# A three-layer block: recurrence with early parameter columns, seams by blocks, turned narrow projections and another order in the first attention

## The chip, the cores and the metric

The kernel runs on one core of one Trainium2 chip. The metric is the device time of one execution in microseconds. TensorE multiplies, VectorE, ScalarE and GpSimd work elementwise, SyncE issues most transfers; each engine runs its own list of instructions in order, and they wait for one another by semaphores. Three runs of the kernel before took 1351.91, 1352.85 and 1360.21 us, median 1352.85.

## The reference, cut to what matters

256 tokens of width 1024, float32, batch 1. Three layers in a row.

```
# layer 1: complex diagonal recurrence (32 groups, 16 channels, 64 states), then an MLP
u = rms(h) @ w_in                      # 1024 -> 512
x[t] = a * x[t-1] + B u[t]             # complex, per group; a, B from lam, dt
y = Re(C x) + d * u
z = gelu(y); z = z * sigmoid(z @ w_glu); mix = z @ w_out
h = h + rms(mix)
h = h + rms(relu(rms(h) @ w1)**2 @ w2) # 1024 -> 4096 -> 1024
# layer 2: attention over selected keys, then an MLP of the same shape
q, k, v, qi, ki, wi = split(rms(h) @ w_in)   # 1024, 256, 256, 512, 64, 8 columns
q, k, qi, ki = rope(each)
score[t, s] = sum_heads relu(qi . ki) * wi   # 8 heads
keep the 64 keys of highest score (causal); softmax attention, 16 heads on 4 of k, v
h = h + rms(o @ w_out); h = h + rms(MLP(rms(h)))
# layer 3: one projection (z, conv part, dt: 32 columns, q, k, v, gates), a chunked
# state recurrence and three dilated window attentions side by side, then a conv FFN
dt = softplus(proj_dt + bias)
```

## The kernel before, in words

Activations are kept as two blocks of 128 tokens (`tb`). Every weight comes in **pieces** of 1 MB, each of two halves a and b, by SyncE into `raw` (two buffers). ScalarE copies a half rounded into `HI` (`hi_next`, `hi_to`), and the difference raw - HI goes to `LO`: half a by VectorE (`lo_next`, `lo_to`), half b by GpSimd (`upto`), both by `low_part`; `lo_both` is VectorE doing both. `HI` and `LO` have four slots; a slot is free when TensorE signals `piece_done`, and a buffer of `raw` is free when the difference of the piece two before is taken. A product is three matmuls (`three`: high x high, high x low, low x high). Activations are split in the same way after being turned: TensorE transposes `y` in four quarters (block, half of the columns) into PSUM (`norm_transpose`), ScalarE takes the high part `XH` (`xT_high`), VectorE the low part `XL` (`xT_low`).

The order of the work is written out by hand, one list for each engine; `keep_busy` puts matmuls on zeros between, here called fillers. No planner orders anything.

**Recurrence** (0 to 107 us). VectorE makes the tables from the parameters: powers, then `w5` (B times powers), angles and their fraction of a turn in `e5`, `cq5` (C times powers). Parameters that lie in rows are turned into columns (`late_columns`, in the middle of `inputs_turned`). TensorE projects u in two pieces (`ch_major`), ScalarE reorders it (`to_steps`) and copies the turned tables (`inputs_out`), takes sine and cosine. TensorE makes `kernels5` and four `drive`s; VectorE scans four groups (`scanned`); `within` and `carried` give y; ScalarE's gelu, then `glu` and the down projection.

**Seam** between two layers: `post` squares the result (ScalarE), scales it (VectorE), takes the power -0.5 (GpSimd, `row_rstd`) and adds it to `h`; `pre` squares h, takes the power and writes `y`. In the kernel before, `post` runs over both token blocks, then `pre` over both, then the four quarters. TensorE has 20 fillers ahead of the transposes and 2 between the blocks. The last down piece of an MLP signals `acc_first` when its token block 0 is complete.

**First attention**. Pieces from number 37 (`P_ATT`): two for the index queries, a narrow one of 72 columns (ki, wi: the tail), two for k and v, two and two for q, four for the output. `tok_major` with n < 128 runs 48 matmuls of n columns with four fillers. The index scores of block 0 are summed and its 64 largest found (8 turns of MAX8 and MATCH_REPLACE8), then those of block 1; `rotate_keys` comes before, `rotate_queries(0)` between. Twelve jobs follow (`JOBS1`): scores, masked maximum (`largest1`), exponential, division (`normed1`), transpose, weighted sum.

**Start of layer 3**. Nine projections c of two pieces each for q, v, k, each 48 matmuls of 512 columns, into PSUM banks `bank2(c)`; c = 0 and c = 1 share banks 0 and 1, since the narrow dt projection (32 columns, piece 84) has bank 2. `head_norm` normalises q and k heads; `softplus` follows c = 0.

## Time and profile before

| | |
|---|---|
| median of 3 runs | 1352.85 us |
| profiled execution | 1348.93 us |
| its span | 1347.1 us |
| TensorE busy | 1299.1 us (96%) |
| VectorE busy | 985.8 us (73%) |
| ScalarE busy | 667.3 us (50%) |
| GpSimd busy | 434.8 us (32%) |
| mean granted clock | 0.991 |

The times of the trace are counted from the first instruction; the profiled execution's own time is 1.8 us longer than its span. A busy TensorE can be running fillers. A granted clock of 1.00 is 2.4 GHz, 0.50 is 1.2 GHz; a stretch between them holds both. A matmul's duration in a row is its latency, matmuls overlap: their spacing is read from the starts.

### The profile page before, as it was taken

How to read it: one execution, taken by the hardware profiler on the slowest of the kernel's cores; microseconds unless marked ns; L12 is line 12 of the kernel's file. 1: busy time of each engine (PE TensorE's matmuls, PEld its weight loads, DVE VectorE, ACT ScalarE, POOL GpSimd, SP SyncE). 2: the span in 40 equal slices, each digit the busy share in tenths (PEclk: the TensorE clock that was granted, in tenths of full speed). 3: DMA queues.
4: the chain of work that ended last, by engine and by line, in shares of the span. 5: the costliest groups of instructions: out<-in, count | busy, mean ns of one | idle time of the engine just before them, and what ended most of it. 6: DMA issues, size and time to landing. Idle time of an engine off the chain costs nothing.

```text
span 1347.1 us, 21106 instructions
## 1 busy us (share of the span) xinstructions
PE 1299.1 (96%) x7798; PEld 1101.8 (82%) x7798; DVE 985.8 (73%) x1486; ACT 667.3 (50%) x1119; POOL 434.8 (32%) x213
## 2 busy tenths in 40 slices
PE   6999999999999999999999999999999979999998
PEld 6876888878667788887888888899999947899998
DVE  7977777676964755556665645499999985699997
ACT  5755444444464544445354544355555523455553
POOL 3005444544201555554354322210000002345553
PEclk9999999999889999999899999999999999999999
DMA  7026665645203566663465533354454314366663
GB/s 227 17 85 200 189 197 184 190 134 188 94 32 125 157 191 189 191 193 108 156 209 162 151 94 95 92 150 136 141 155 141 125 63 141 90 191 189 187 187 109
DMA packets 166363, 197.12 MB, mean 146 GB/s; under 512 B 9981, under 2 KB 131325, under 8 KB 166269
## 3 DMA queue, kind: packets, MB, share of 16 engines
q1 hardware_dynamic: 164939, 191.54, 46.4%
q10 hardware_dynamic: 1362, 4.74, 1.0%
q8 instruction: 40, 0.66, 0.2%
q14 instruction: 22, 0.18, 0.0%
HBM read 195.20 MB, written 1.05 MB: 146 GB/s over the span
## 4 chain that ended last, share of the span: by engine, by line
PE 71%; DVE 20%; issue 3%; ACT 3%; DMA 1%; POOL 1%; DVEq 0%; SPq 0%; ACTq 0%
PE acc L639 21%; PE wk L594 9%; PE wk L571 7%; PE wk L573 7%; PE wk L572 7%; PE wk L596 4%; DVE LO L1844 4%; DVE arena L2376 2%; PE acc L618 2%; PE wk L1075 1%; PE acc L571 1%; PE acc L1101 1%; PE acc L572 1%; PE acc L573 1%; DVE arena L2375 1%
## 5 line engine op out<-in xcount | busy, mean ns | idle before, releaser
L447 POOL TENSOR_TENSOR LO<-raw,HI 128x1024 fp32r<-128x1024 f32 (+1 forms) x160 | 401.1, 2512 | 830.9 <-ACT HI L1320 789.3
L1320 ACT ACTIVATE HI<-raw 128x1024 fp32r<-128x1024 f32 (+3 forms) x382 | 364.5, 996 | 115.7 <-DMA raw<-in_w_in 27.4
L447 DVE TENSOR_TENSOR LO<-raw,HI 128x1024 fp32r<-128x1024 f32 (+1 forms) x160 | 221.6, 1388 | 114.3 <-ACT HI L1320 113.9
L571 PE MATMUL wk<-X,HI 128*128 128x256 f32 x784 | 224.6, 286 | 2.0 <-DVE X L1877 1.2
L572 PE MATMUL wk<-X,HI 128*128 128x256 f32 x784 | 221.7, 283 | 0.0
L573 PE MATMUL wk<-X,LO 128*128 128x256 f32 x784 | 221.7, 283 | 0.0
L594 PE MATMUL wk<-X,HI 128*128 128x512 f32 x512 | 182.3, 399 | 2.5 <-DVE X L1877 2.5
L571 PEld LDWEIGHTS wk<-X,HI 128*128 128x128 f32 x784 | 150.2, 192 | 5.0 <-issue 2.8
L572 PEld LDWEIGHTS wk<-X,HI 128*128 128x128 f32 x784 | 150.3, 192 | 0.9
L573 PEld LDWEIGHTS wk<-X,LO 128*128 128x128 f32 x784 | 150.2, 192 | 0.0
L596 PE MATMUL wk<-X,LO 128*128 128x256 f32 x512 | 143.5, 280 | 0.0
L639 PE MATMUL acc<-HI,HH 128*128 128x512 f32 x424 | 131.9, 392 | 3.8 <-DVE HL L2419 3.1
L639 PE MATMUL acc<-LO,HH 128*128 128x512 f32 x424 | 131.0, 390 | 0.0
L639 PE MATMUL acc<-HI,HL 128*128 128x512 f32 x424 | 130.8, 390 | 0.0
L594 PEld LDWEIGHTS wk<-X,HI 128*128 128x128 f32 x512 | 96.2, 188 | 26.4 <-issue 2.9
L596 PEld LDWEIGHTS wk<-X,LO 128*128 128x128 f32 x512 | 96.6, 189 | 1.1
L571 PE MATMUL wk<-HI,X 128*128 128x512 f32 (+2 forms) x240 | 93.3, 389 | 1.6 <-DVE arena L2303 1.5
L639 PEld LDWEIGHTS acc<-LO,HH 128*128 128x128 f32 x424 | 79.6, 188 | 17.3
L639 PEld LDWEIGHTS acc<-HI,HL 128*128 128x128 f32 x424 | 79.6, 188 | 17.0
L572 PE MATMUL wk<-LO,X 128*128 128x512 f32 (+2 forms) x240 | 91.1, 380 | 0.0
L573 PE MATMUL wk<-HI,X 128*128 128x512 f32 (+2 forms) x240 | 91.1, 379 | 0.0
L639 PEld LDWEIGHTS acc<-HI,HH 128*128 128x128 f32 x424 | 75.4, 188 | 18.8 <-DVE HL L2419 4.0
(364 smaller groups left out, 2158.1 us busy)
## 6 DMA issues: line engine op xcount, KB each, us to landing
raw<-in_mlp_w SPq DMA_DIRECT2D x128, 512.0 KB, 4.0
raw<-in_w_in SPq DMA_DIRECT2D x100, 512.0 KB, 3.9
raw<-in_w_up SPq DMA_DIRECT2D x44, 512.0 KB, 3.9
raw<-in_w_down SPq DMA_DIRECT2D x44, 256.0 KB, 3.1
raw<-in_att_w_in SPq DMA_DIRECT2D x16, 512.0 KB, 4.4
raw<-in_w_ssd_proj SPq DMA_DIRECT2D x16, 512.0 KB, 4.2
raw<-in_att_w_out SPq DMA_DIRECT2D x8, 512.0 KB, 4.4
raw<-in_w_out SPq DMA_DIRECT2D x8, 512.0 KB, 4.3
```

Of the source, the lines that this page charges most:

```text
L447: tensor_tensor(LO[:, s, cs], raw[:, s % 2, "ab".index(part), 0:m], HI[:, s, cs].bitcast(F32), ALU.subtract).then_inc(S(f"lo_{part}"), 1)
L571: mm(o, lh, rh, start=start, stop=False, skip_group_check=skip)
L572: mm(o, lh, rl, start=False, stop=False, skip_group_check=skip)
L573: return mm(o, ll, rh, start=False, stop=stop, skip_group_check=skip)
L594: mm(o, HI[:, s, w:w + P], X2[:, k, :, :].rearrange("p r t -> p (r t)"), start=k == 0, stop=False, skip_group_check=True)
L596: last = mm(o[:, 0:SEQ], LO[:, s, w:w + P], XH[:, k, :], start=False, stop=k == KD - 1, skip_group_check=True)
L618: mm(o, zero_bf[:, 0:P], zero_bf[:, :], start=True, stop=True, skip_group_check=True)
L639: last = mm(acc[:, tb, n * 512:(n + 1) * 512], lhs[:, ts], w[:, s, c:c + 512], start=begin, stop=end, skip_group_check=True)
L1075: last = mm(wkf[:, o:o + K], qT2[hs, gi * 4 + hd // 2, tb * P:(tb + 1) * P], kT2[hs, gi * 4 + hd // 2, 0:K], start=True, stop=True)
L1320: A(HI[:, s, j * m:(j + 1) * m], raw[:, s % 2, j, 0:m], ACT.Copy).then_inc(S(f"hi_{part}"), 1)
L1844: TT(LO[:, s, cs], raw[:, s % 2, "ab".index(part), :], HI[:, s, cs].bitcast(F32), ALU.subtract).then_inc(S(f"lo_{part}"), 1)
L2376: STT(o, x, taps[j][k], o, ALU.mult, ALU.add)
```

## The change

Four things, in one diff.

**Recurrence.** GpSimd waits for the first turned activations before its half of piece 0 and takes both halves of piece 1. VectorE computes the small tables ahead of `xT_low(0)`; all four products of `w5` come before the four sums. The columns are turned ahead of the second projection. The products `kernels5` are cut in halves, one ahead of the last six `inputs_turned`, one behind `drive(0)`. ScalarE copies `cq5` into place; VectorE makes the third copy in `e5`. ScalarE's order becomes u, columns, u, both `inputs_out`. Fillers are fewer: 130 before, 101 after.

**Seams behind both MLPs.** `post` and `pre` go block by block; the last two down pieces run block 0 of both, then block 1 of both; block 0's transposes and projection come before block 1's transposes.

**Turned narrow projections.** The 72 and the 32 columns become the stationary operand, 24 matmuls of 256 columns, and are transposed back.

**First attention.** k, v and q projections of the tail's successors are cut by token block; both blocks' scores are summed before the keys are rotated; four `rel` buffers; jobs 0 and 1 begin inside the search of block 1; second query half rotated inside jobs 0 and 1. GpSimd waits at four places for VectorE's rotations. In layer 3, c = 1 has its own banks and `softplus` follows c = 3.

```diff
 gpsimd, recurrence
+            pool.wait_ge(S("xT_hi"), 1)
             upto(0)
+            pool.wait_ge(S("lo_a"), 1)
+            pool.wait_ge(S("tables5"), 1)
+            low_part(pool, G.tensor_tensor, Ring().at(1), "a", 2048)
+            upto(1)
 gpsimd, first attention
-            row_rstd(3)
-            row_rstd(4)
+            row_rstd(3, 4)
+            upto(P_ATT + 4)
+            pool.wait_ge(S("ki_roped"), 2)
+            upto(P_ATT + 6)
+            pool.wait_ge(S("lo_a"), P_ATT + 8)
+            upto(P_ATT + 8)
+            pool.wait_ge(S("q_roped"), 2)
+            upto(P_ATT + 10)
+            pool.wait_ge(S("q_roped"), 4)
             upto(P_ATT + 14)
 tensor
+            def ch_narrow(s, o, n):
+                for k in range(KD):
+                    last = three(o, HI[:, s, k * n:(k + 1) * n], LO[:, s, k * n:(k + 1) * n], XH[:, k, :], XL[:, k, :],
+                                 k == 0, k == KD - 1)
+                return last
+            def back_turned(src, dst, n):
+                for tb in range(TB):
+                    last = nc.tensor.transpose(dst(tb), src[:, tb * P:(tb + 1) * P], ident[0:n, 0:n])
+                return last
...
             pe.wait_ge(S("ct_ready"), 1)
+            pe.wait_ge(S("cols_ready"), 2)
-            keep_busy(spare5, 4)
-            for g in range(8):
+            keep_busy(spare5, 2)
+            inputs_turned(0)
+            inputs_turned(1)
+            keep_busy(spare5, 2)
+            pe.wait_ge(S("w5_ready"), 2)
+            kernels5(0)
+            for g in range(2, 8):
                 inputs_turned(g)
                 keep_busy(spare5, 2)
...
+            drive(0)
+            keep_busy(spare5, 2)
+            pe.wait_ge(S("dd5_ready"), 1)
+            kernels5(1)
+            for q in range(1, 4):
+                keep_busy(spare5, 1)
                 drive(q)
...
-            for q, n in enumerate((0, 4, 10, 10)):
+            for q, n in enumerate((0, 1, 2, 5)):
                 keep_busy(spare5, n)
                 carried(q)
-            keep_busy(spare5, 8)
+            keep_busy(spare5, 5)
...
-            keep_busy(spare5, 14)
+            keep_busy(spare5, 7)
             glu(glu_slot, 2)
...
-            norm_transpose(2, 20, 2)
-            proj1(0, 0, 2)
-            proj1(0, 1, 2)
+            norm_transpose(2, 14, 0, (0, 1))
+            slots = [arrived(), arrived()]
+            for tb in range(TB):
+                if tb == 1:
+                    norm_transpose(2, 0, 0, (2, 3))
+                for part in range(2):
+                    last = tok_block(slots[part], wk[:, tb, :], tb, 4 * part, 4, 512, part == 0, part == 1, 2)
...
             s = arrived()
-            used(tok_major(s, lambda tb: wk[:, 2 + tb, 0:ATT_TAIL], 0, KD, ATT_TAIL, True, True))
+            used(ch_narrow(s, accf[0:ATT_TAIL, 1024:1024 + SEQ], ATT_TAIL))
+            s = arrived()
+            tok_block(s, wk[:, 2, :], 0, 0, 4, 512, True, False)
+            pe.wait_ge(S("tail_read"), 1)
+            back_turned(tailT, lambda tb: tail1[:, tb, 0:ATT_TAIL], ATT_TAIL).then_inc(S("tail_psum"), 1)
+            used(tok_block(s, wk[:, 3, :], 1, 0, 4, 512, True, False))
 scalar, first attention
+            hi_to(P_ATT + 4)
+            done(P_ATT + 2)
+            A(tailT, accf[0:ATT_TAIL, 1024:1024 + SEQ], ACT.Copy).then_inc(S("tail_read"), 1)
             hi_to(P_ATT + 6)
             tile_evac(0, qiT[:, :, 0:P])
 vector
+            def by_block(j, e, n):
+                scaled(j, e, 0)
+                residual(e, 0)
+                pre_block(n, e + 1, 0)
+                scaled(j, e, 1)
+                xT_low(n, (0, 1))
+                residual(e, 1)
+                pre_block(n, e + 1, 1)
+                xT_low(n, (2, 3))
...
+            summed(0)
+            summed(1)
+            rotate_keys()
+            lo_to(P_ATT + 7)
+            searched(0)
+            lo_to(P_ATT + 8)
+            rotate_queries(0)
+            searched(1, first_jobs)
             for n in range(N1 + 1):
                 if n + 2 < N1:
                     largest1(n + 2)
-                if n in (N1 - 2, N1 - 1):
+                if n < TB:
+                    rotate_queries(1, (n,))
+                if n in (2, 3, N1 - 2, N1 - 1):
                     lo_next()
-                if n + 1 < N1:
+                if 1 <= n < N1 - 1:
                     normed1(n + 1)
```

ScalarE's `by_block` has the order: squares of the result for block 0, of h for block 0, of the result for block 1, `xT_high` of quarters 0 and 1, squares of h for block 1, `xT_high` of quarters 2 and 3.

## Rows read from the trace of the kernel before

**Rows 1.** The page: busy time by engine; shares of the chain that ended last.
```profile
PE 1299.1 (96%) x7798; PEld 1101.8 (82%) x7798; DVE 985.8 (73%) x1486; ACT 667.3 (50%) x1119; POOL 434.8 (32%) x213
...
PE 71%; DVE 20%; issue 3%; ACT 3%; DMA 1%; POOL 1%; DVEq 0%; SPq 0%; ACTq 0%
```
**Rows 2.** Stretches of TensorE: length, busy, granted clock, DMA share, GB/s.
```profile
298.00:306.60 8.60, 7.48 (x40) 1.00 0.00 1
360.70:370.90 10.20, 9.81 (x34) 0.54 0.01 2
650.70:657.50 6.80, 5.31 (x23) 0.57 0.01 2
654.54:667.54 13.00, 13.00 (x50) 0.85 0.11 26
```
**Rows 3.** Timeline of VectorE, recurrence: start us, duration us, line, form, idle before.
```profile
15.72 2.22 DVE L1928 TENSOR_TENSOR arena<-arena 128x16 f32<-128x16 f32 x1
...
26.47 2.36 DVE L1844 TENSOR_TENSOR LO<-raw,HI 128x1024 fp32r<-128x1024 f32 x2
...
57.75 0.69 DVE L2036 TENSOR_TENSOR arena<-wk,arena 128x512 f32<-128x512 f32 x1 [1.23 <-PE wk L720]
...
79.46 2.35 DVE L1844 TENSOR_TENSOR LO<-raw,HI 128x1024 fp32r<-128x1024 f32 x2
```
**Rows 4.** Timeline of GpSimd, recurrence.
```profile
15.56 2.35 POOL L447 TENSOR_TENSOR LO<-raw,HI 128x1024 fp32r<-128x1024 f32 x1 [4.37 <-ACT HI L1320]
```
**Rows 5.** Timeline of ScalarE, recurrence: second `to_steps`, second gelu.
```profile
44.53 4.46 ACT L1399 ACTIVATE y<-wk 32x128 f32<-32x128 f32 x16
...
82.61 4.47 ACT L1456 ACTIVATE arena<-acc 32x128 f32<-32x128 f32 x16 [2.65 <-PE acc L748]
```
**Rows 6.** Timeline of TensorE, recurrence: `kernels5`, `drive`, last `carried`, fillers ahead of `glu`.
```profile
47.24 0.97 PE L730 MATMUL acc<-arena 128*128 128x32 f32 x8
...
60.04 1.90 PE L720 MATMUL wk<-y,arena 128*128 128x64 f32 x16
...
80.68 1.89 PE L748 MATMUL acc<-arena 128*128 128x63 f32 x16
...
87.44 3.19 PE L618 MATMUL acc<-zero_bf 128*128 128x512 bf16 x14
```
**Rows 7.** Timeline of VectorE: last hidden low part of the first MLP.
```profile
289.97 0.69 DVE L2114 TENSOR_TENSOR HL<-arena,HH 128x512 fp32r<-128x512 f32 x1 [0.70 <-ACT HH L1489]
```
**Rows 8.** Timeline of TensorE: first matmul behind the first seam.
```profile
306.60 0.47 PE L571 MATMUL wk<-HI,X 128*128 128x512 f32 x1
```
**Rows 9.** Stretches of TensorE: 48 matmuls of 256 columns; the 72-column tail.
```profile
22.00:27.86 5.86, 5.86 (x51) 1.00 0.51 183
317.60:323.60 6.00, 6.00 (x54) 1.00 0.60 177
```
**Rows 10.** Timeline of TensorE: first matmul of c = 1.
```profile
654.54 0.79 PE L571 MATMUL wk<-HI,X 128*128 128x512 f32 x1 [1.49 <-DVE arena L2303]
```
**Rows 11.** Timeline of ScalarE behind the seam: pieces 39 and 40, then 41.
```profile
307.54 2.68 ACT L1320 ACTIVATE HI<-raw 128x288 fp32r<-128x288 f32 x4 [0.33 <-issue]
314.75 1.06 ACT L1320 ACTIVATE HI<-raw 128x1024 fp32r<-128x1024 f32 x1 [4.53 <-DMA raw<-in_att_w_in]
```
**Rows 12.** Timeline of TensorE: query transposes; transposes of the fifth job.
```profile
360.68 1.17 PE L859 MATMUL acc<-cst,arena 128*128 128x128 f32 x8 [2.68 <-ACT arena L1522]
...
393.80 0.66 PE L939 MATMUL acc<-cst,arena 128*128 128x128 f32 x4
```
**Rows 13.** Timeline of VectorE: query rotation until the next sum; search of block 1.
```profile
353.22 0.68 DVE L453 TENSOR_TENSOR y<-wk,cst 128x512 f32<-128x512 f32 x1
...
357.44 0.35 DVE L2192 TENSOR_SCALAR arena<-arena,wi_s 128x256 f32<-128x256 f32 x1
...
361.80 0.43 DVE L2200 MAX8 top<-arena 128x8 f32<-128x256 f32 x1
...
369.67 0.29 DVE L2203 TENSOR_SCALAR arena<-arena 128x256 bf16<-128x256 f32 x1
```

More of the change, by code:

```diff
@@ L87, in next, with at @@
         return s, k, n
+    def at(self, n):
+        while self.n < n:
+            self.next()
+        return self
     def enter(self, i, per_slot):
@@ L602, in tok_major, with tok_block @@
                 for tb in range(TB):
-                    for k in range(kt):
-                        ts = slice(tb * P, (tb + 1) * P)
-                        if norm is not None:
-                            xT_wait(norm, tb, k0 + k)
-                        if n < P and k % 4 == 0:
-                            keep_busy(accf[:, 1536:2048], 1)
-                        last = three(outs(tb), XH[:, k0 + k, ts], XL[:, k0 + k, ts], HI[:, s, k * n:(k + 1) * n],
-                                     LO[:, s, k * n:(k + 1) * n], start and k == 0, stop and k == kt - 1)
+                    last = tok_block(s, outs(tb), tb, k0, kt, n, start, stop, norm)
                     if tb == 0 and first:
                         last.then_inc(S(first), 1)
+                return last
+            def tok_block(s, o, tb, k0, kt, n, start, stop, norm=None):
+                ts = slice(tb * P, (tb + 1) * P)
+                for k in range(kt):
+                    if norm is not None:
+                        xT_wait(norm, tb, k0 + k)
+                    last = three(o, XH[:, k0 + k, ts], XL[:, k0 + k, ts], HI[:, s, k * n:(k + 1) * n],
+                                 LO[:, s, k * n:(k + 1) * n], start and k == 0, stop and k == kt - 1)
                 return last
@@ L643, in down, with norm_transpose @@
                 return last
-            def norm_transpose(n, meanwhile=0, between=0):
+            def norm_transpose(n, meanwhile=0, between=0, quarters=range(4)):
                 keep_busy(wk[:, 3, :], meanwhile)
-                for q in range(4):
+                for q in quarters:
                     tb, b = q // 2, q % 2
@@ L722, in drive, with kernels5 @@
                 last.then_inc(S("bu_psum"), 1)
-            def kernels5():
-                for i in range(ST):
-                    if i % 2 == 0:
-                        keep_busy(spare5, 1)
+            def kernels5(half):
+                for i in range(8 * half, 8 * half + 8):
+                    keep_busy(spare5, 1)
                     for r in range(2):
@@ L839, in mlp @@
                 mlp_up(MC - 1, 1)
[L840 to L841 removed]
+                slots = []
+                for tb in range(TB):
+                    for par in range(2):
+                        if tb == 0:
+                            pe.wait_ge(S("hid_lo"), MC - 1 + par + base)
+                            slots.append(arrived())
+                        ts = slice(tb * P, (tb + 1) * P)
+                        for kk in range(2):
+                            for lhs, w, end in ((HH, HI, False), (HH, LO, False), (HL, HI, par == 1 and kk == 1)):
+                                for n in range(2):
+                                    c = kk * 1024 + n * 512
+                                    last = mm(acc[:, tb, n * 512:(n + 1) * 512], lhs[:, par, kk, ts], w[:, slots[par], c:c + 512],
+                                              start=False, stop=end, skip_group_check=True)
+                        if tb == 1:
+                            used(last)
+                    if tb == 0:
+                        last.then_inc(S("acc_first"), 1)
             mlp(0)
[L846 removed]
+            norm_transpose(2, 14, 0, (0, 1))
             def proj1(bank, part, norm=None):
@@ L1869, in pre, with xT_low @@
                     pre_block(n, e, tb)
-            def xT_low(n):
-                for q in range(4):
+            def xT_low(n, quarters=range(4)):
+                for q in quarters:
                     tb, b = q // 2, q % 2
```

335 lines of the change are left out of this document (186 added, 149 removed).

## The prediction, made blind

> **What bounds the kernel.** I read the page first: TensorE is busy 96% of the span and holds 71% of the chain that ended last, VectorE 20% [rows 1]. Matmuls set the time nearly everywhere, so only places where TensorE waits, runs fillers (`keep_busy`) or has its clock lowered can give anything. The stretches by window show where: the granted clock is 0.54 to 0.57 (for most of the stretch the lower level, 1.2 GHz) in a stretch of 10 us of the first attention and in one of 7 us at the start of layer 3; at the seams it stays at the upper level, 2.4 GHz [rows 2]. Then the timelines of each engine, for five places: the recurrence (0 to 107 us), two seams (298 and 627 us), the first attention (307 to 430 us) and the two narrow projections in it and behind 646 us. In the recurrence VectorE runs from 10 to 80 us with hardly a pause: the reader sees it wait for TensorE's drives (1.23 us), the longest of its pauses there [rows 3]. The MLPs, the second attention and the chunked recurrence are untouched; what is gained ahead of them should arrive at the end, since they are bound by TensorE.
>
> **Recurrence, -4.7 us (bounds -1 and -6).** Removed from VectorE: two differences of piece 1 (2.3 us) and a stall in which a subtraction on 16 elements took 2.22 us while GpSimd subtracted 1024 columns [rows 3, 4]. GpSimd now waits for the first turned activations (about 17.1 us) and then subtracts 0b; a VectorE instruction with two SBUF operands stops for it again, for about 1 us. So I get: small block from 15.9 to 20.5, low parts of the activations and piece 0 to 24.1, powers (2.8 us) to 26.9, where the tables before began at 28.9. GpSimd's two halves of piece 1 (2.4 us each) run to about 33. The first four table products read PSUM, which the rows show unhindered; the four sums behind them lose some 1.5 us. Tables, angles and inner products then end at about 51.
>
> That is not what the scans wait for. Piece 0 is projected 24.2 to 30, the late columns and eight fillers reach 32, piece 1 runs 33.1 to 38.9 (both projections at 5.8 us). ScalarE takes 4.5 us for u's second half [rows 5], then eight copies paced by TensorE, for half of the kernel products (8 x 0.6 us, from four of them in 0.8 [rows 6] and a filler each) stand between: to 51.0; absolute value, sine, cosine (3.1 us) to 54.1; VectorE's added copy 0.7 us to 54.9. Before, the first scan began at 57.75. The second needs drive 1, now behind the second half of the products: 51.0 + 1.7 for drive 0, 0.4 fillers, 5.0 products, 1.0 skip term, 0.2, 1.7 for drive 1 [rows 6] = 61.0 us. Three scans of 5.43 us follow: 77.4 instead of 79.5 us. Fewer fillers (10 + 10 ahead of the last two `carried` become 2 + 5, 14 ahead of the third glu group become 7) let TensorE follow at once: last `carried` ends at 79.7 instead of 82.4, ScalarE's second gelu (4.5 us) and copy at 84.8, low part at 85.5, third glu group at 85.6 instead of 90.3 [rows 5, 6]. That is 4.7 us, and the down projection inherits it. The four copies of `cq5` moved to ScalarE (4 us) lie before the products' end, in its free time. If they or the sine chain end later than I have them, the gain shrinks to 1.
>
> **Seams, -1.0 each (bounds +1 and -3).** The last two down pieces are run block by block: block 0 is complete 24 matmuls (5.5 us) before the end instead of 12, but its second half needs the last hidden low part, which ends at 290.66 [rows 7] where TensorE would be at 289.8: 0.9 us of wait, MLP end 299.0. Block 0: squares, power, residual, squares, power, product: y at 300.6. Fourteen fillers (3.0 us) hold TensorE to 302.0 and hide it. Transposes, ScalarE's and VectorE's copies: first matmul at 303.75 instead of 306.60 [rows 8]. But block 1's residual now stands on VectorE behind block 0's low parts: its y comes at 308.8, its activations at 311.1, while block 0's 24 matmuls end at 309.3. Turning, 0.9 us more wait, 5.6 us: 316.7 instead of 317.7. The second seam has the same instructions.
>
> **Narrow projections: -3.0 in the attention, -6.7 with what follows in layer 3.** 48 matmuls of 72 or 32 columns take 0.11 us each whatever their columns, with four fillers 6.0 us; 48 matmuls of 256 columns take 5.8 us [rows 9]. Turned: 24 of these, 2.9 us, and two transposes, 0.3: -3.0 for 72 columns, -3.3 for 32, which began to run at the low clock. ScalarE's copy lies beside the next matmuls. Bounds: no gain, and -4. Behind 646 us two things go as well: c=1 no longer waits for head_norm 0 (1.49 us [rows 10]), since its banks are free, and its 48 matmuls no longer start at the low clock (13.0 us [rows 2] against 11.1 between seam and tail [rows 8, 9], -1.9). Softplus (9 us of VectorE) moves to c=3, where VectorE has only differences; pieces lead by three there. Total here -6.7; bounds -4 and -8.
> What the Trainium skill says speaks against turning: by "TensorE: Matmul & The Clock Gate", section "Back-to-back issue gap", an isolated matmul costs its streamed columns, N/2.4 + 2.5 ns with a floor near 25, so 1.2 us before and 2.6 us after; the same section says that a stream with weight loads is slower than that at small N, and the 0.11 us above agree with the latter.
>
> **First attention, -4.6 with its tail's 3.0 (bounds +3 and -6).** The 3.0 us won in the tail are at once at risk. HI of pieces 39 and 40 was taken right behind the seam at 307.5; now ScalarE is in the seam until 311. Piece 41 can load when 39 is split, 43 when 41 is; ScalarE takes 43 ahead of the first evacuation. Pieces took 3.5 to 6 us from a freed buffer, with two in flight [rows 11]: I get HI 43 ready at about 329, where TensorE stands at 326.5: 2.8 us of wait. Then key projection and index products to 342, last value half 344.7. VectorE sums both blocks' scores first (to 344.4) and only then turns the keys (3.3 us, to 347.7): 3.0 us of wait for TensorE, the successor of the 2.68 us before the query transposes [rows 12]. From there VectorE is the chain: difference 1.2, search of block 0 6.3, difference 1.2, queries 4.1 (360.5), search of block 1 8.6 [rows 13] with the first two jobs inside (3.6), two query rotations and three maxima: third job's product ready at 379.8 instead of 382.2. Two differences stand in jobs 2 and 3 now, but late_queries comes a job later, when its input is there. Fifth job's transposes: 388.2 instead of 393.8 [rows 12], -5.6 against before, of which 1.0 is the seam's: -4.6. From job 4 on both kernels take 3.0 us a job.
>
> **Sum**: 4.7 + 1.0 + 4.6 + 1.0 + 6.7 = 18.0 us. The profiled run took 1348.93 us, 0.3% under the median of 1352.85: 1331 on its scale, **1335 us** for a median.
>
> **Rivals.**
> 1. *The ring starves the attention* (0.20). The wait for piece 43 and the one for the keys are each as long as the 2.68 us behind which the clock fell for 10 us before. Cold stretches on the chain, at 0.43 instead of 0.22 us a matmul, take 3 to 5 us: attention gives 0, sum 13: 1340. For: the chain of loads. Against: all of it is worked out from landings in one profile.
> 2. *ScalarE becomes the recurrence's bound* (0.12): sine behind the eight copies, scans at 57 again, 1 us there: 1339.
> 3. *The narrow matmuls cost their columns* (0.02): at 0.23 us for 512, 32 columns cost 0.014, 48 of them 0.7 us, turned 2.8: two gains of 3.2 become losses of 2.1: 1346. Rows 9 speak against. This is the skill's rule for the isolated gap.
> 4. *Better than worked out* (0.12): seams whose y overtakes the fillers and a piece 43 in time, some 1.5 + 1.5 + 4: 1328.
> 5. *Slower* (0.04): of 130 fillers in the recurrence 29 go. If the clock falls there at about 50 us and stays at half to 105, then the 11 us of down, 5.8 of glu and some 8 of `within` and `carried` double: +25 - 18 = +7, 1360. It decides if the granted clock is low for over 40 us ahead of the MLP. Against: the seams, with as many gaps, stay at 1.00 [rows 2].
>
> **Numbers.** My forecast 0.50 (own range 1330 to 1340). The range 1325 to 1346 takes in rivals 1 to 4 and the bounds. A change of over 1% is 13.5 us, about what this measurement tells from none: faster 0.72 (forecast, rival 4 and some of 1 and 2), same 0.25, slower 0.03.
>
> **What would show it.** Recurrence: first scan at 55, second at 61, first matmul of the MLP 5 us earlier. Seams: TensorE's first block projection 4.8 us behind the last down matmul and a second wait near 1 us. Attention: an idle of TensorE ended by ScalarE's first evacuation, one ended by VectorE's key rotation. Second block: no clock under 1.00 at 645. Wrong if the recurrence gives under 2 us, or if attention's tail gain is kept whole.

## The result: 5.3 to 8.5 us faster, where 18 were forecast

Eight runs of the changed kernel have a median of **1344.15 us** (1341.87 to 1347.69), eight of the kernel before beside them 1352.69 us: ratio 0.9938, 95% interval 0.9909 to 0.9967. A second comparison (e1, below) gave medians 5.3 us apart and 0.9964 (0.9949 to 0.9978). The time lies in the range 1325 to 1346, but the gain is under half of the 18.0 us of the sum, and with under 1% it falls where the prediction had put a chance of 0.25 ("same"), not 0.72. One execution of e5 (3654 us) and one of the kernel before beside e13 to e15 (1370 us) were disturbed and are in no ratio. The profiled execution is the slowest of its eight: 1347.69 us, span 1345.8, against 1347.1 before. It shows where gains arise and go, not their median size.

The page: TensorE is as busy as before, VectorE has 38 us more (not more work: the same 160 splits of one group take 1.65 instead of 1.39 us on average, 263 us instead of 222), and TensorE's share of the chain went from 71% to 68% [rows 1].

```profile
PE 1286.8 (96%) x7700; PEld 1096.1 (81%) x7700; DVE 1024.0 (76%) x1483; ACT 670.9 (50%) x1124; POOL 419.1 (31%) x215
...
PE 68%; DVE 21%; ACT 4%; issue 3%; DMA 2%; POOL 1%; DVEq 0%; SPq 0%; ACTq 0%
```

Stretches of the changed kernel (bounds, length, busy time of PE, PEld, DVE, ACT, POOL, granted clock, DMA share, GB/s). First the first MLP's start, then the first attention behind its narrow projection and three parts of it, layer 3 from its first projection to the second attention, and the latter's start.

```profile
113.00:123.00 10.00, 8.77 (x41) 7.11 (x41) 6.32 (x7) 5.56 (x7) 5.82 (x2) 0.83 0.73 231
...
317.20:438.30 121.10, 108.07 (x532) 82.19 (x531) 76.82 (x221) 58.17 (x130) 28.31 (x13) 0.93 0.32 103
325.00:332.00 7.00, 5.01 (x20) 4.01 (x21) 1.45 (x1) 2.49 (x5) 2.85 (x2) 0.76 0.87 278
347.50:363.00 15.50, 15.43 (x63) 12.93 (x64) 14.54 (x46) 5.53 (x7) 7.29 (x4) 0.80 0.44 137
384.00:396.00 12.00, 9.50 (x53) 7.31 (x54) 5.50 (x19) 7.65 (x20) 2.34 (x1) 0.84 0.44 166
646.20:750.90 104.70, 102.17 (x513) 85.94 (x511) 77.88 (x134) 56.01 (x68) 48.35 (x19) 1.00 0.61 191
...
750.00:762.00 12.00, 10.81 (x52) 9.15 (x53) 7.01 (x14) 5.42 (x11) 2.45 (x1) 0.72 0.42 117
```

The waits of TensorE in the changed kernel (what waited, what ended it, total, times, longest). The three with one occurrence of 3.5, 3.3 and 2.5 us are all in the first attention; before, its one long wait was 2.68 us [rows 12].

```profile
PE acc L921 <- DVE arena L474: 3.5, 1, 3.5
PE acc L921 <- ACT arena L1630: 3.3, 1, 3.3
PE acc L1018 <- DVE arena L2355: 3.2, 3, 1.9
...
PE wk L664 <- ACT arena L1665: 2.5, 1, 2.5
```

Set side by side, the start of each stage tells where time goes. In us from the span's start, read from the timelines of TensorE; "again" is the changed kernel's second trace:

```
                                     before   changed   again
recurrence, down projection starts    97.51    92.65    92.49
first MLP, first matmul              119.47   114.73   114.49
  its second projection              125.80   122.61   120.91
first MLP, last down matmul ends     298.1    296.0    294.4
layer 2, first projection ends       317.7    314.4    312.7
narrow projection ends               323.7    317.2    315.6
attention's output ends              438.3    438.2    440.1
layer 3, first projection ends       646.5    646.1    648.1
second attention starts              756.4    750.9    755.0
span                                1347.1   1345.8   1347.3
```

The changed kernel is 6.5 and 8.1 us ahead behind the narrow projection, and level and 1.8 us late at the end of the attention. All that is won before 317 us is lost in that one stretch: 114.6 us before, 121.1 and 124.5 now. Layer 3 then gives 5.2 and 3.1 us. From the start of the second attention to the end, where nothing was changed, both traces lose again: 590.7 us before, 594.9 and 592.3 now. Of the fifteen other traces (the kernel before and e2 to e15), thirteen have 590.6 to 590.9 and two (e10, e15) 592.2. The second attention's first 12 us run at clock 0.72 in the first trace, at 0.86 in e1, e10 and e15, at 1.00 in the rest. So part of what the first trace lacks is chance.

### The profile page after: what moved, and what is told of

Read it like the earlier page. It is cut to its first block, busy times and chain, and to the rows that moved or that the text cites. A ratio compares the mean times of both kernels' runs of the same rounds, so it can differ in the third digit from the quotient of the medians.

```text
span 1345.8 us, 20924 instructions
## 1 busy us (share of the span) xinstructions
PE 1286.8 (96%) x7700; PEld 1096.1 (81%) x7700; DVE 1024.0 (76%) x1483; ACT 670.9 (50%) x1124; POOL 419.1 (31%) x215
## 3 DMA queue, kind: packets, MB, share of 16 engines
q1 hardware_dynamic: 164939, 191.54, 46.1%
## 4 chain that ended last, share of the span: by engine, by line
PE 68%; DVE 21%; ACT 4%; issue 3%; DMA 2%; POOL 1%; DVEq 0%; SPq 0%; ACTq 0%
PE acc L685 20%; PE wk L637 9%; PE wk L601 6%; PE wk L603 6%; PE wk L602 6%; PE wk L639 5%; DVE LO L1948 4%; DVE arena L2517 2%; PE wk L1163 1%; PE acc L601 1%; PE acc L898 1%; PE acc L1189 1%; PE acc L602 1%; PE acc L603 1%; DVE LO L462 1%
## 5 line engine op out<-in xcount | busy, mean ns | idle before, releaser
L462 POOL TENSOR_TENSOR LO<-raw,HI 128x1024 fp32r<-128x1024 f32 (+1 forms) x162 | 387.5, 2398 | 847.6 <-ACT HI L1408 770.1
L462 DVE TENSOR_TENSOR LO<-raw,HI 128x1024 fp32r<-128x1024 f32 (+1 forms) x160 | 263.3, 1648 | 97.8 <-ACT HI L1408 97.5
L685 PE MATMUL acc<-HI,HH 128*128 128x512 f32 x392 | 122.1, 393 | 3.8 <-DVE HL L2560 3.1
L685 PE MATMUL acc<-LO,HH 128*128 128x512 f32 x392 | 121.3, 390 | 0.0
L685 PE MATMUL acc<-HI,HL 128*128 128x512 f32 x392 | 121.0, 390 | 0.0
L601 PE MATMUL wk<-HI,X 128*128 128x512 f32 x208 | 84.1, 404 | 4.2 <-DVE X L1981 4.2
L685 PEld LDWEIGHTS acc<-LO,HH 128*128 128x128 f32 x392 | 73.6, 188 | 15.9
L685 PEld LDWEIGHTS acc<-HI,HL 128*128 128x128 f32 x392 | 73.6, 188 | 15.8
L2239 DVE TENSOR_TENSOR HL<-arena,HH 128x512 fp32r<-128x512 f32 x32 | 84.0, 2626 | 2.8 <-ACT HH L1601 2.8
L602 PE MATMUL wk<-LO,X 128*128 128x512 f32 x208 | 82.4, 396 | 0.0
```

What stands on the lines that cost most here:

```text
L462: tensor_tensor(LO[:, s, cs], raw[:, s % 2, "ab".index(part), 0:m], HI[:, s, cs].bitcast(F32), ALU.subtract).then_inc(S(f"lo_{part}"), 1)
L601: mm(o, lh, rh, start=start, stop=False, skip_group_check=skip)
L602: mm(o, lh, rl, start=False, stop=False, skip_group_check=skip)
L685: last = mm(acc[:, tb, n * 512:(n + 1) * 512], lhs[:, ts], w[:, s, c:c + 512], start=begin, stop=end, skip_group_check=True)
L2239: TT(HL[:, par, :, :], sq_b[:, par, :].rearrange("p (j t) -> p j t", j=2), HH[:, par, :, :].bitcast(F32), ALU.subtract).then_inc(S("hid_lo ...
```

## The experiments

Two places are given for each: the **attention stretch** (end of the narrow projection to the end of the output) and **layer 3** (end of its first projection to the start of the second attention). Before: 114.6 and 109.9. The ratios are to the kernel before on the same chip.

### e1: the changed kernel again

> The changed kernel once more, nothing altered: a second trace of it, to see which stretches of low clock belong to a place and which come and go. Theory A (the gain is lost in the first attention, by waits that the order of the work makes): the stretch from the last matmul of the narrow projection (317.2 us) to the last matmul of the attention's output (438.4) is again 121 us long, 6 us longer than in the kernel before (114.9), with the same three waits of TensorE of about 3.3, 3.5 and 2.5 us. Theory B (the gain is eaten by chance drops of the clock, other ones in each execution): the stretches of low clock at 114, 752, 1087 and 1097 us lie elsewhere or are missing, and the span is up to 5 us shorter. Both can hold. Ratio to the kernel before 0.994.

Measured: 1344.44 us, ratio 0.9964 (0.9949 to 0.9978); 124.5 and 106.8 us. The three waits return, 3.2, 3.5 and 2.5 us. The low clock at 114 us does not: the MLP's first projection takes 5.9 us and not 7.3. The one at 752 us does, weaker (0.86 against 0.72). Both theories hold in part. The attention's loss belongs to the place, 6.5 to 9.9 us; which stretches outside it run at the lower level changes from one execution to the next.

Four more traces below leave the first attention as it is in the changed kernel: 120.8 (e6), 124.5 (e7), 123.4 (e9) and 124.7 us (e14). So an edit there is told from chance by a single trace only outside 120.8 to 124.7. Layer 3, unaltered in e1 to e6 and e8, takes 104.7 to 107.4.

What a wait costs depends on the clock too. Behind the 2.5 us this trace (timeline of TensorE: start, duration, line, form, idle before) has two jobs at the doubled time:

```profile
389.03 0.38 PE L664 MATMUL wk<-zero_bf 128*128 128x512 bf16 x1 [2.50 <-ACT arena L1665]
389.33 2.07 PE L1009 MATMUL wk<-arena 64*128 64x128 f32 x8
391.33 1.11 PE L1018 MATMUL acc<-cst,arena 128*128 128x128 f32 x4
392.38 1.97 PE L1032 MATMUL acc<-arena 128*64 128x128 f32 x8
...
394.82 2.07 PE L1009 MATMUL wk<-arena 64*128 64x128 f32 x8
```

The score matmuls take 2.07 us where they take 1.16 at the upper level, and the next job's come 5.5 us later instead of 3.0.

### e2, e3, e4: the three waits, one edit each

```diff
 # e2 (VectorE); e3 has it too
             summed(0)
-            summed(1)
             rotate_keys()
             lo_to(P_ATT + 7)
+            summed(1)
 # e3 in addition (ScalarE)
-            hi_to(P_ATT + 6)
+            hi_to(P_ATT + 5)
             tile_evac(0, ...); tile_evac(1, ...); tile_evac(2, ...)
+            hi_to(P_ATT + 6)
 # e4 (ScalarE, alone)
+                if n == 3:
+                    late_queries()
                 if n in (3, 6):
                     hi_next()
-                if n == 3:
-                    late_queries()
```

> VectorE turns the keys and splits the next piece between the two sums of index scores instead of behind both. Theory A: TensorE's wait of 3.5 us ahead of the key transposes (344.1 to 347.6) is gone, the search of block 0 begins 2 to 3 us earlier because the idle time of VectorE inside the second sum is filled, the following 48 matmuls are no longer at the low clock (13.3 to 11.1 us), and the fourth job's transposes come 3 to 5 us earlier; what is left of it at the end of the attention is less, since the fifth job still waits for the late queries: 1 to 4 us. Theory B: no gain, because the wait returns ahead of the query transposes. Ratio 0.991 under A, 0.994 under B.

Measured: 1347.61 us, ratio 0.9971 (0.9943 to 1.0); 128.8 us, longer by 4 than the longest above. The wait ahead of the keys is gone and returns ahead of the query transposes as 5.47 us, with a granted clock of 0.50 from 360 to 370 us. Theory B, and worse than "no gain".

> As the one with the keys first, and ScalarE evacuates the three index transposes before it splits piece 43. Theory A: TensorE's wait of 3.3 us behind the index transposes at 323.7 is gone, and the 12 matmuls behind it take 3.0 us and not 4.1; the index products start 4 us earlier, the sums follow, and the fourth job's transposes come 6 to 9 us earlier than in the changed kernel. Theory B (the ring of pieces sets the pace): the split of 43 only comes a microsecond later and with it pieces 45 to 48, so that TensorE waits as long ahead of the query projections. Ratio 0.988 under A, 0.993 under B.

Measured: 1342.44 us, ratio 0.995 (0.9931 to 0.9968); 120.0 us. The wait behind the index transposes is 0.34 us, the third job's transposes come at 375.1 instead of 379.5 us; 5.46 us of wait ahead of the queries remain. The stretch is 4.5 us shorter than in e1 but only 0.8 under the shortest of the unaltered ones, and the fourth job's transposes came 3.7 us earlier (380.1) where 6 to 9 were expected. Theory A holds for the wait; its size is not shown here. Against e2, which lacks only this edit, the stretch is 8.8 us shorter.

> In the fourth turn of the job loop ScalarE evacuates the late queries before it splits a piece, not behind it. Theory A: TensorE's wait of 2.5 us (387.8 to 390.3) shrinks to about 0.7, the low clock behind it (390 to 393 us) is gone, the fifth job's transposes come 3 us earlier (389 instead of 392.1) and the end of the attention's output 2 to 3 us earlier. Theory B: the jobs behind are bound by VectorE or by GpSimd's split, so that the end of the output stays at 121 us behind the narrow projection. Ratio 0.992 under A, 0.994 under B.

Measured: 1342.86 us, ratio 0.9943 (0.9927 to 0.996); 120.7 us, 3.8 under e1, but no less than e6 has without this edit. The wait is 1.27 us and not the 0.7 expected; e3 and e6, which leave ScalarE's order alone here, have 1.27 and 1.57; the changed kernel, e1, e7, e9 and e14 have 2.5 to 3.7. Fourth to fifth job is still 7.1 us (382.6 to 389.7; 7.0 to 8.4 in the unaltered traces). ScalarE's order is at most a part of this wait; no gain of this edit is shown.

### e5: late queries a job earlier

```diff
 # TensorE: behind the third job, not the fourth
-                if n == 3:
+                if n == 2:
                     late_queries()
 # ScalarE: ahead of copies1(3), not behind hi_next
```

> The late queries are transposed a job earlier, as in the kernel before (behind the third job's transposes and second product), and ScalarE evacuates them ahead of that job's copy. Theory A (the move of this step to the fourth job took its slack: the very next scores need it): no wait of TensorE over 1 us there; from the fourth to the fifth job's transposes 3.0 to 3.5 us instead of 7.0 and 7.5, no low clock behind it, and the attention's output 4 to 6 us earlier measured from the end of the narrow projection (117 us instead of 121.1 and 124.5). Theory B (VectorE or GpSimd bound these jobs): the wait turns up at another job and the stretch stays above 120 us. Ratio 0.991 under A, 0.996 under B.

Measured: 1341.26 us, ratio 0.9899 (0.9865 to 0.9934); 116.9 us, 3.9 under the shortest unaltered one. Theory A, with the number expected: no wait of TensorE over 1 us is left there. Fourth and fifth job's transposes are 3.0 us apart, though this group of late transposes itself still ran at the low clock:

```profile
379.65 1.97 PE L993 MATMUL wk<-cst,arena 128*128 128x128 f32 x8
...
383.43 0.66 PE L1018 MATMUL acc<-cst,arena 128*128 128x128 f32 x4
384.02 1.09 PE L1032 MATMUL acc<-arena 128*64 128x128 f32 x8
385.36 1.16 PE L1009 MATMUL wk<-arena 64*128 64x128 f32 x8 [0.25 <-issue]
386.44 0.66 PE L1018 MATMUL acc<-cst,arena 128*128 128x128 f32 x4
```

### e6: fewer fillers at the seams

```diff
-            norm_transpose(2, 14, 0, (0, 1))     # and (4, 14, ...)
+            norm_transpose(2, 8, 0, (0, 1))      # and (4, 8, ...)
```

> 8 instead of 14 fillers ahead of the first block's transposes at the two seams. In the trace of the changed kernel block 0 of y is ready 1.75 us behind the last down matmul, and the fillers hold TensorE to 3.04. Theory A (the seam gave 0.2 instead of 1.0 us because too many fillers stand in it): the transposes start at 1.75, and the first projection of layer 2 and of layer 3 end 17.1 us behind the last down matmul instead of 18.4: 1.2 us each, ratio 0.994. Theory B (fewer fillers, more idle time, and the clock falls): a granted clock under 1.00 behind the seam, and 1 to 3 us lost: ratio 0.998.

Measured: 1338.99 us, ratio 0.9877 (0.9829 to 0.9925); 120.8 and 104.7 us. The first projection ends 17.2 us behind the last down matmul instead of 18.4, at clock 1.00. The transposes start 2.9 us behind the down matmuls in the changed kernel and 1.6 here:

```profile
295.44 1.68 PE L664 MATMUL wk<-zero_bf 128*128 128x512 bf16 x7
296.95 1.04 PE L701 MATMUL wk<-cst,y 128*128 128x128 f32 x8
299.20 0.47 PE L601 MATMUL wk<-HI,X 128*128 128x512 f32 x1 [1.21 <-DVE X L1981]
```

Theory A in the trace. That the median fell by more than the 2.4 us (0.994 was expected) is not explained; its interval is 13 us wide.

### e7, e9, e14: the wait behind c=2 in layer 3

```diff
 # ScalarE: e7 moves hi_to(last2(1) + 3), three pieces, behind the square; e9 the last piece only:
-                hi_to(last2(c) + 3)
+                hi_to(last2(c) + (2 if c == 1 else 3))
 ...
+                if c == 1:
+                    hi_to(last2(c) + 3)
 # VectorE, e14 in addition to e9
-                lo_to(last2(c) + 3)
+                lo_to(last2(c) + (2 if c == 1 else 3))
                 if not 3 <= c < 6:
                     head_norm(c)
+                if c == 1:
+                    lo_to(last2(c) + 3)
```

> At the start of layer 3 ScalarE squares the projection of c=1 as soon as it is complete, and splits the next pieces behind that. In the traces of the changed kernel the square waited 5.5 us for two transfers that stand ahead of it in ScalarE's order, and TensorE then waited 1.6 and 2.1 us ahead of the transposes behind c=2. Theory A (order on ScalarE): that wait is gone, and c=3 starts 1.6 to 2 us earlier. Theory B (VectorE, which loses 2.3 us to GpSimd in one small instruction, sets it): the wait stays above 1 us. Ratio 0.995 under A, 0.9965 under B.

Measured: 1350.34 us, ratio 0.9954 (0.9919 to 0.9989); layer 3 takes 110.0 us. The wait is gone, and another of 4.36 us stands ahead of c=2's own matmuls, ended by GpSimd's share of their piece: I had moved two pieces that TensorE needed. A miss of the edit, not a verdict on the theory.

> As the square first, but ScalarE still splits two of the three pieces ahead of the square of c=1 and only the third, for which it waited 7.4 us on the transfer, behind it. Theory A (one transfer that nobody needs yet stands ahead of the square): the square starts within 1 us of the end of c=1's projection, c=2's projection does not wait as it did when all three were put behind (4.4 us), TensorE's wait of 1.6 to 2.7 us ahead of the transposes behind c=2 is under 0.3, and the second attention starts 104.5 us or less behind the first projection of layer 3 (before: 109.9, changed kernel: 104.7 and 106.8). Theory B (the collision of VectorE's small instruction with GpSimd alone holds the chain): wait still above 1 us. Ratio 0.9945 under A.

Measured: 1345.55 us, ratio 0.9942 (0.9916 to 0.9969); 106.7 us. The square starts with the end of c=1's projection, and TensorE still waits 1.96 us, where theory A had under 0.3. VectorE had the same late piece ahead of its norm: its split, at 664.6 us, follows an idle of 3.9. GpSimd's subtraction, theory B's cause, is there too: it holds one instruction of the norm for 2.38 us instead of 0.17.

> The changed kernel; at c=1 of layer 3 both ScalarE's square and VectorE's norm stand ahead of the split of the third piece. Theory A (the late piece stands ahead of the norm on two engines): norm of c=1 ready 7 to 9 us behind the end of c=1's projection instead of 13.6, TensorE's wait behind c=2 under 0.3 us, and the second attention 104.5 us or less behind the first projection of layer 3. Theory B (GpSimd's subtraction stops VectorE's small instructions for 2.3 us wherever they stand): the wait is shorter only where no subtraction falls into the norm. Ratio 0.994.

Measured: 1341.25 us, ratio 0.9917 (0.9889 to 0.9945); 102.9 us, no wait behind c=2. ScalarE of e14: the square, then 2.49 us of idle time for the transfer, which nobody waits for any more.

```profile
661.57 1.03 ACT L1731 ACTIVATE y<-wk 128x1024 f32<-128x1024 f32 x1 [3.92 <-PE wk L603]
665.09 1.06 ACT L1408 ACTIVATE HI<-raw 128x1024 fp32r<-128x1024 f32 x1 [2.49 <-DMA raw<-in_w_in]
```

VectorE of e14: the norm of c=1 is complete at 667.5, 6.1 us behind that projection (13.7 in the changed kernel). Theory A gives these numbers, but theory B is not excluded: no subtraction fell into this norm, while in the changed kernel and in e9 one did, for 2.1 and 2.2 us, more than the wait. And e10 below, with e9's order only, shows no wait and 102.9 us as well (e11 and e12, with the same order there: 106.7 and 104.4). The order helps; how much of the wait was the order's and how much GpSimd's is not told apart.

```profile
662.63 1.22 DVE L2442 TENSOR_REDUCE arena<-y 128x16 f32<-128x1024 f32 x1 [0.30 <-ACT y L1731]
...
666.19 1.29 DVE L2446 TENSOR_TENSOR arena<-wk,arena 128x512 f32<-128x512 f32 x2
```

### e8: the waits filled

```diff
+            keep_busy(accf[:, 1024:1536], 14)    # ahead of tile_transpose(2)
+            keep_busy(accf[:, 0:512], 15)        # ahead of the wait for k_roped
+                        keep_busy(wk[:, n % 2, :], 10)   # seventh job, ahead of q1T_read
```

> The changed kernel with 14, 15 and 10 fillers in the three long waits of the first attention (ahead of the key index transposes, of the key transposes, and of the seventh job's scores); no order is changed. Theory A (the waits themselves cost, the clock behind them little): the stretch from the narrow projection to the end of the attention's output stays at 121 to 125 us. Theory B (the low clock behind the waits is a large part): granted clock 1.00 or nearly so from 320 to 400 us, no matmul group at the doubled time, and the stretch 4 to 6 us shorter (118). Ratio 0.996 under A, 0.992 under B.

Measured: 1341.34 us, ratio 0.9891 (0.9843 to 0.9939); 120.0 us. From 320 to 360 us the clock is 1.00, where the changed kernel has 0.76 and 0.80, and still the stretch is hardly shorter (0.8 us under the shortest unaltered one): up to the third job VectorE sets the pace, whose product comes 62.8 us behind the narrow projection, within the 60.8 to 64.0 of the unaltered traces. The clock falls again around 360 and 390:

```profile
361.00:371.00 10.00, 9.68 (x41) 7.64 (x42) 8.45 (x38) 4.78 (x18) 2.33 (x2) 0.83 0.01 2
384.00:394.00 10.00, 9.95 (x55) 7.15 (x56) 5.25 (x19) 6.95 (x17) 2.36 (x1) 0.82 0.43 161
320.00:360.00 40.00, 38.48 (x193) 27.87 (x195) 27.80 (x80) 17.28 (x23) 11.89 (x5) 1.00 0.43 132
```

Between the theories: 1 to 4.5 us under the two traces of the changed kernel, not 4 to 6. I read it so that the low clock costs something only where TensorE is the bound, from the fourth job on; this run does not prove it, since the clock fell there again.

### e10, e11, e12, e15: the mends together

e10 is the changed kernel with the evacuation of e3, e5, e6 and e9. e11 adds e2's order of VectorE, e12 the order of before instead (`searched(0)` and the queries ahead of `summed(1)`), e15 is e12 with e14.

> Four edits on the changed kernel together: index transposes evacuated ahead of the split of piece 43, late queries a job earlier, 8 fillers at the two seams, square of c=1 ahead of the third piece. Each removes a wait at its own place, so the gains should add: 3 to 4 us for the late queries with the clock behind them, 1 to 4 for the evacuation (VectorE starts its sums 4 us earlier), 1.2 twice at the seams, 2 in layer 3. Theory A (the losses are these four waits): attention's output 112 to 114 us behind the narrow projection, ratio 0.982 to 0.985, some 1331 us. Theory B (chance drops of the clock eat what waits give back): ratio 0.988 and new low stretches at other places.

Measured: **1334.11 us**, ratio 0.9857 (0.9815 to 0.9899); 113.0 and 102.9 us. Theory A.

> The four mends, and VectorE turns the keys between its two sums. Theory A (VectorE is the bound from the first index product to the third job, so that the order of its work only moves TensorE's wait from the key to the query transposes): the third job's transposes come within 1 us of where they come with the four mends alone, and TensorE shows one wait of about 5.5 us instead of a wait ahead of the keys and none ahead of the queries; the longer wait is followed by more low clock, so it is equal or up to 3 us slower. Theory B (the keys hold the chain): 2 to 3 us faster.

Measured: 1333.34 us, ratio 0.9858 (0.9815 to 0.9901); 116.5 us with one wait of 5.47. Longer by 3.5, and theory B is out. Theory A had the wait, but not that the third job too is later by 3.5 instead of under 1: behind the query transposes at the low clock VectorE waits 1.96 and 1.50 us for the first scores, where e10 has 0.68 and 0.48. The execution times show no difference from e10.

> The four mends with VectorE's order of before: sum of block 0, keys, search of block 0, queries, then sum and search of block 1. Theory A (the order itself is worth nothing, VectorE does the same work without idle time either way): third job's transposes within 1 us of the four mends alone, but TensorE waits less ahead of the keys and queries, less low clock: equal to 2 us faster. Theory B (summing both blocks first is what brought the third job 4.7 us forward in the changed kernel): the third job 3 us or more later than with the four mends.

Measured: **1332.61 us**, ratio 0.9852 (0.9809 to 0.9895); 113.0 us. TensorE waits neither for keys nor for queries, and the stretch is as long as with both sums first: theory A in the result. The third job is 1.5 us earlier, counted from the narrow projection (58.5 against 60.0), not within 1; at the fifth it is gone (67.0 in both). Summing both blocks first gave nothing.

> The four mends with VectorE's order of before in the attention, and the norm of c=1 ahead of the third piece. Theory A: as the four mends with the old order (ratio 0.985), 1 us less for the wait behind c=2: 0.984 to 0.985, some 1331 us. Theory B: no difference from it, since the wait there was 1.2 us in one trace and none in another.

Measured: 1333.72 us, ratio 0.9862 (0.9812 to 0.9912); 114.2 and 102.9 us. No difference from e12 that the runs tell. e10, e11, e12 and e15 all beat both kernels, by 10 us and more; among them the runs don't choose.

### e13: the recurrence alone

The recurrence's part of the change on the kernel before, nothing else.

> The kernel before with the recurrence part of the change alone (its order on TensorE, ScalarE, VectorE and GpSimd, and its fillers). Theory A (the term of 4.7 us is real and arrives at the end): down projection of the recurrence at 92.5 instead of 97.5 us, the MLP's end 5 us earlier, ratio 0.9964, some 4.8 us. Theory B (the fillers taken out lower the clock behind the recurrence, and part is lost again): the first projection of the MLP at the low clock in part of the runs, ratio 0.9975 or more.

Measured: 1346.8 us, the medians 5.0 us apart; the ratio 0.9949 (0.9916 to 0.9982) says some 7 us, 2 to 11. In the trace the first MLP ends 5.9 us earlier than before (292.2) and the attention's output 3.2 (435.2), the clock being 0.91 from 310 to 330 us. The term arrives, and the attention, whose order is that of the kernel before, takes back 2.6 us of it. So that order has two traces, 114.6 and 117.2 us, both under the 120.8 to 124.7 of the new one.

## Why the prediction was wrong, by its own steps

**The failed step** is in the first attention: "late_queries comes a job later, when its input is there". It was costed at nothing. The seventh job's scores, the first that need these queries, stand right behind it in TensorE's order, so that the step now had no job between itself and its user: 8 transposes, the split of a piece that ScalarE had ahead of the evacuation (2.0 us), the evacuation (1.1). ScalarE of the changed kernel:

```profile
387.05 2.00 ACT L1408 ACTIVATE HI<-raw 128x1024 fp32r<-128x1024 f32 x2
389.07 1.09 ACT L1665 ACTIVATE arena<-wk 128x512 f32<-128x512 f32 x2
```

The attention's times in the prediction are without the recurrence's gain, so distances have to be compared, not moments. From the third job's product to the fifth's transposes it had 8.4 us (379.8 to 388.2). The kernel before takes 11.6, from the end of this product on VectorE to the row of 393.80 [rows 12]:

```profile
381.54 0.69 DVE L2228 TENSOR_TENSOR arena<-arena,small 128x512 f32<-128x512 f32 x1
```

and the changed kernel 11.5, from the end of the first of these rows (VectorE) to the start of the last (TensorE):

```profile
379.85 0.69 DVE L2355 TENSOR_TENSOR arena<-arena,small 128x512 f32<-128x512 f32 x1
...
385.11 0.66 PE L1018 MATMUL acc<-cst,arena 128*128 128x128 f32 x4
...
392.09 1.11 PE L1018 MATMUL acc<-cst,arena 128*128 128x128 f32 x4
```

In e1 it takes 11.9, in e6, e7, e9 and e14 11.4 to 12.0. Nothing of the 3.2 us came. e5, which moves this step with its evacuation back and nothing else, takes 8.6.

These 3.1 to 3.5 us are not the whole miss. The stretch was forecast at 113.0 us (114.6 less 1.6) and took 121.1 and 124.5, 8.1 and 11.5 too long. Another 3.3 and 3.8 us came up to the third job's product, forecast 60.1 us behind the narrow projection and measured 63.4 and 63.9. And 1.7 and 4.3 came behind the fifth job's transposes, where the forecast had 3.0 us a job for both kernels: 44.6 us before, 46.3 and 48.9 now, with jobs at the doubled times. e5 and e10 still have 46.1.

**The two other waits** were forecast at 2.8 and 3.0 us and measured 3.3 and 3.5. That part was seen, but the low clock behind them only as a rival. e10 against e5 shows what the first cost, a split ahead of an evacuation when VectorE, the bound until the third job, could not start: the third job's product comes 60.0 us behind the narrow projection instead of 62.3, and the stretch is 3.9 us shorter (one trace each). Taking away the second wins nothing: in e2 and e11 it returns ahead of the queries, and the third job is later, not earlier.

**Rival 1** (waits bring the low clock, the attention gives 0, 1340 us) had a part of the mechanism, and too small a price. It let the attention give 0 instead of 4.6, narrow projection included. The narrow projection gave 3.2, the rest took 6.5 and 9.9. By the Trainium skill, "TensorE: Matmul & The Clock Gate", section "What's actually happening", how many matmuls run at the lower clock at a kernel's start differs from run to run of one kernel. These traces show the like in a kernel's middle, of which the page does not speak: 7.3 and 5.9 us for the same projection.

**Recurrence**, -4.7: measured -4.9 and -5.0 at its down projection (the clock is 1.00 from 50 to 105 us). The steps inside held: first scan at 54.4 (forecast 54.9), second at 60.9 (61.0), last `carried` ends at 79.4 (79.7), third glu group at 85.5 (85.6). VectorE and TensorE here, as in rows 3 and 6:

```profile
54.38 0.69 DVE L2159 TENSOR_TENSOR arena<-wk,arena 128x512 f32<-128x512 f32 x1
...
60.94 0.69 DVE L2159 TENSOR_TENSOR arena<-wk,arena 128x512 f32<-128x512 f32 x1 [1.04 <-PE wk L763]
```

```profile
59.01 1.89 PE L763 MATMUL wk<-y,arena 128*128 128x64 f32 x16
...
77.49 1.89 PE L792 MATMUL acc<-arena 128*128 128x63 f32 x16
```

Rivals 2 and 5 did not occur.

**Seams**, -1.0 each: -0.2 each. The wait for the hidden low part was 0.79 (forecast 0.9), the second one 0.98 (0.9), the first matmul came 5.1 us behind the down matmuls (4.75). From there to the projection's end my sum had 13.0 us and the trace 13.3. The MLP itself, from its second projection to its end, became 1.1 us longer (forecast 0.9). Small slips of one sign, 0.2 + 0.3 + 0.3, used up the gain. The fillers are no slip of the sum: it had them at 3.0 us, and y at 1.6 behind the down matmuls (3.04 and 1.75 measured). But "hide" was the wrong word for it: they hold TensorE 1.3 us longer than y needs, and e6 takes that back, 1.2 us that the forecast never had.

**Narrow projections**: turned, 24 matmuls took 2.8 us instead of 6.0 (forecast -3.0, measured -3.2); in layer 3, 2.7 us. Rival 3 is out. The stretch of 32 columns turned, and c=1 behind it, which lost both the wait [rows 10] and the low clock [rows 2]:

```profile
646.00:648.90 2.90, 2.90 (x26) 2.76 (x25) 1.22 (x1) 2.40 (x3) 0.32 (x1) 1.00 0.96 355
...
648.70:659.80 11.10, 11.10 (x52) 8.94 (x50) 9.94 (x16) 4.99 (x6) 7.08 (x3) 1.00 0.37 105
```

At the end of c=1's projection 7.4 us were won by the first of the two traces. Then 1.6 to 2 us were given back to a wait that I had not seen: everything had moved 7 us closer to the transfers, the norm stood behind a split whose transfer was now late, and GpSimd's subtraction fell into it. Result 5.2 and 3.1 instead of 6.7; 7.0 in e14.

**The sum** of 18.0 us is reached only by other kernels: with the four mends the gain is 18.2 us (e10), with the old order too 19.7 (e12), both against 1352.26, and some 2.4 of it are e6's, which were in no forecast. In the attention stretch they reach 113.0 us, 1.6 under before, just what the prediction had for it without the tail. That is luck in part: it had this number with a wait of 2.8 us that e10 and e12 do not have, and in e12 without the order of the sums that was to bring it.

For the profiled execution the account closes. The forecast's 1331 us is a span of 1329.1; 1345.8 is 16.7 more: 8.1 in the attention, 4.2 behind the start of the second attention, 1.6 at the seams, 1.5 at the first MLP's low clock, 1.5 in layer 3, less 0.2 in the tail. The median of the eight is 3.5 us below this execution, so not all of it is in a typical one.

## What to carry to other kernels

A step that is moved later "because its input is there" has to be costed at its other end: who is the first to need its output, and what stands ahead of it on the engine that passes it on. A gain ahead of a stage bound by another engine turns into waits there, and the clock can add to them: behind the wait of 3.3 us 12 matmuls took 4.1 us instead of 3.0, behind that of 2.5 us a job in e1 took 5.5 instead of 3.0. A split for a piece that is not yet needed should stand behind an evacuation or a norm that is waited for, on every engine that shares the split; e7 shows that moving two pieces too many is harmful (a new wait of 4.36 us); e9 and e14 point to both engines being needed, though e10 went without.

## What the runs showed of the hardware

The stretches at the lower clock come and go between executions of one program even behind short waits: in e1 the clock is 1.00 from 113 to 123 us, 0.83 in the first trace, with the same 1.23 us of wait ahead of it. Over all 17 traces of this case that projection takes 7.2 to 7.5 us in four (the changed kernel, e7, e10, e11) and 5.6 to 6.0 in thirteen, from its first matmul to the fillers behind it. The second attention starts behind waits of 0.97 and 0.33 us, at clock 1.00 or at 0.72 (the changed kernel and e5). The low clock costs 1.5 us at the first of these places; the stretch from the second attention on differs by up to 4.3. That is why one profile is not enough for changes of this size.

VectorE's instructions on 16 elements again stopped while GpSimd subtracted 1024 columns, now inside the norm that TensorE waited for. Instructions with an operand in PSUM were not stopped: the norm's last two products took 1.29 us in the changed kernel with a subtraction beside them (from 672.67) and 1.29 in e14 with none. VectorE of the changed kernel, 0.17 us for the same instruction elsewhere:

```profile
669.65 2.27 DVE L1959 TENSOR_TENSOR arena<-arena 128x16 f32<-128x16 f32 x1
```

The Trainium skill has this in "SBUF — State Buffer", section "SBUF: two separate sides": the pair of ports is held for a whole instruction. GpSimd's subtraction ran from 669.46 for 2.44 us, which agrees.
